# A partner swap moved from DMA to TensorE, a score matmul cut in two, a bias matmul on 33 rows: one kernel, two layers

## The reference

```python
# first layer: the relative bias, one row per head
off = np.arange(3 * blk)[None, :] - blk - np.arange(blk)[:, None]
bt = rel_bias[_t5_bucket(off * dil)]            # 32 buckets, 12 heads
...
# second layer: rotary positions on 16 of the 64 channels of q and k
x1, x2 = xr[..., : ROT_DIM // 2], xr[..., ROT_DIM // 2:]
rot = jnp.concatenate([x1 * c - x2 * s, x2 * c + x1 * s], axis=-1)
...
# second layer: scores of 128 queries, masked by chunks of 64 keys
scores = jnp.einsum('bqhmd,bkhmd->bhmqk', qb, kb).astype(jnp.float32) * scale
scores = jnp.where(mask[None, None, None], scores, -jnp.inf)
p = jax.nn.softmax(scores, axis=-1)
w = p[:, :, 0] - lam * p[:, :, 1]
```

## Time and profile before

| what | value |
|---|---|
| median of 3 runs | 3016.0 us (3014.78 to 3016.84) |
| profiled execution, its own time | 3014.78 us |
| its span, first to last instruction | 3012.7 us |
| TensorE matmuls busy | 2937.9 us, 98% |
| VectorE / ScalarE / GpSimd busy | 52% / 36% / 12% |
| mean granted TensorE clock | 0.996 |

### The profile page before, as it was taken

The page is one execution under the profiler, slowest core; times in us unless marked ns, Lnnn a source line. Parts: engine busy times, 40 slices in busy tenths (PEclk is TensorE's granted clock), DMA queues, the critical chain, the costliest instruction groups (busy, mean ns, idle before and its releaser), DMA issues.

```text
span 3012.7 us, 38881 instructions
## 1 busy us (share of the span) xinstructions
PE 2937.9 (98%) x16147; PEld 2493.6 (83%) x16147; DVE 1558.4 (52%) x2184; ACT 1071.6 (36%) x2306; POOL 371.8 (12%) x439
## 2 busy tenths in 40 slices
PE   7999999999999999999999999999999999999998
PEld 5788888888888888888878888888888888888887
DVE  5466666667674224131257555444544478743553
ACT  4443453454443213233332341121112144313553
POOL 0132222332231100000000000000000021101211
PEclk9999999999999999999999999999999999999999
DMA  3211111111012111111363321111111141111101
GB/s 121 74 53 53 43 55 41 46 43 36 26 42 66 50 63 37 66 43 57 116 232 107 125 99 63 43 42 56 44 54 43 56 135 58 71 41 67 41 29 43
DMA packets 60783, 194.33 MB, mean 65 GB/s; under 512 B 8352, under 2 KB 16416, under 8 KB 51392
## 3 DMA queue, kind: packets, MB, share of 16 engines
q1 hardware_dynamic: 58320, 189.19, 18.0%
q10 hardware_dynamic: 2288, 2.67, 0.3%
HBM read 156.80 MB, written 33.98 MB: 63 GB/s over the span
## 4 chain that ended last, share of the span: by engine, by line
PE 91%; DVE 4%; ACT 2%; issue 1%; DMA 1%; POOL 0%; SPq 0%; POOLq 0%; ACTq 0%; DVEq 0%
PE ps L2532 23%; PE ps L2534 23%; PE ps L2533 23%; PE ps L745 3%; PE ps L751 3%; PE ps L1759 1%; PE ps L1722 1%; PE ps L757 1%; PE ps L782 1%; PE ps L776 1%; PE ps L3410 1%; PE ps L788 1%; PE ps L728 1%; PE ps L797 1%; PE ps L796 1%
## 5 line engine op out<-in xcount | busy, mean ns | idle before, releaser
L2532 PE MATMUL ps<-r,r 128*128 128x512 f32 (+4 forms) x2992 | 1165.1, 389 | 20.3 <-DVE ar L3661 5.1
L2534 PE MATMUL ps<-r,r 128*128 128x512 f32 (+4 forms) x2992 | 1111.3, 371 | 0.0
L2533 PE MATMUL ps<-r,r 128*128 128x512 f32 (+4 forms) x2992 | 1108.9, 371 | 0.0
L2532 PEld LDWEIGHTS ps<-r,r 128*128 128x128 f32 (+1 forms) x2992 | 562.4, 188 | 105.6 <-issue 9.7
L2534 PEld LDWEIGHTS ps<-r,r 128*128 128x128 f32 (+1 forms) x2992 | 560.5, 187 | 99.4
L2533 PEld LDWEIGHTS ps<-r,r 128*128 128x128 f32 (+1 forms) x2992 | 562.7, 188 | 79.4 <-issue 0.7
L2532 PE MATMUL ps<-r 128*128 128x512 f32 x512 | 199.7, 390 | 0.8 <-DVE r L2521 0.8
L2534 PE MATMUL ps<-r 128*128 128x512 f32 x512 | 199.2, 389 | 0.0
L2533 PE MATMUL ps<-r 128*128 128x512 f32 x512 | 199.2, 389 | 0.0
L2792 DVE TENSOR_TENSOR ar<-ar,ps 128x512 f32<-128x512 f32 x224 | 150.8, 685 | 89.7 <-PE ps L2534 89.7
L2516 ACT ACTIVATE r<-ar 128x2048 fp32r<-128x2048 f32 x48 | 91.7, 1910 | 275.4 <-PE ps L2534 252.3
(11 more groups left out here) (331 smaller groups left out, 3887.8 us busy)
## 6 DMA issues: line engine op xcount, KB each, us to landing
ar<-wst SPq DMA_DIRECT2D x72, 1024.0 KB, 4.8
ar<-wst SPq DMA_DIRECT2D x56, 512.0 KB, 4.0
ar<-x SPq DMA_DIRECT2D x16, 512.0 KB, 6.0
ar<-sc_g SPq DMA_DIRECT2D x32, 256.0 KB, 4.6
sc_h<-ar SPq DMA_DIRECT2D x32, 256.0 KB, 2.0
sc_x<-ar SPq DMA_DIRECT2D x16, 512.0 KB, 2.7
ar<-sc_x SPq DMA_DIRECT2D x16, 512.0 KB, 3.9
sc_b<-ar SPq DMA_DIRECT2D x24, 260.0 KB, 2.0
```

Of the source, the lines that this page charges most:

```text
L2532: t.do.matmul(o, l[0], r[0], start=first, stop=False)
L2533: t.do.matmul(o, l[0], r[1], start=False, stop=False)
L2534: return t.do.matmul(o, l[1], r[0], start=False, stop=last)
```

## The change

Four edits.

1. The bias matmuls take 33 rows of both operands in place of 128.
2. The partner channels of the rotary step are no longer moved by DMA. A constant 128 by 128 matrix `permT` (one more slice of the `rope` input, loaded in stage 6's queue) holds the swap with its sign, and a new function `rotated` multiplies it with `rp` on TensorE, one matmul of 352, 336 or 512 columns per piece, into banks 4 to 7. VectorE's sine product reads that bank. The sine table loses its sign. The 80 DMAs from ScalarE's queue and the two clears of `rturn` are gone. `rotated` for piece j stands two pieces behind the projection of piece j; the last two stand behind the first and the second value piece.
3. A score cut that crosses the first masked key is cut there too, so that the masked keys have a matmul of their own, and the mask covers exactly that matmul's columns.
4. `lqk` and the tables have a semaphore of their own, `rope_in`.

```diff
@@ pe_bias
-t.do.matmul(bank(6 + n % 2)[:, 0:384], bc(rb[:, n:n + 1], 128, 128), oh[:, n // 4, :], ...)
+t.do.matmul(bank(6 + n % 2)[:, 0:384], bc(rb[0:33, n:n + 1], 33, 128), oh[0:33, n // 4, :], ...)
@@ sp_ff
-sp.do.dma_start(lqk, lam["lqk"].partition_broadcast(P)).then_inc(*lru_in.tick("lqk"))
+sp.do.dma_start(permT, rope[2][:, 0:128]).then_inc(*rope_in.tick("perm"))
+sp.do.dma_start(lqk, lam["lqk"].partition_broadcast(P)).then_inc(*rope_in.tick("lqk"))
@@ rope
+def rope_bank(k):
+    return small_bank(len(lru_keys) + rope_keys.index(k))
+
+def rotated(t, k):
+    i = rope_keys.index(k)
+    t.wait_ge(pj_act, k)
+    t.wait_ge(rope_in, "lqk")
+    if i >= 4:
+        t.wait_ge(rope_dve, ("sin", *rope_keys[i - 4]))
+    w = piece(k)[1]
+    t.do.matmul(rope_bank(k)[:, 0:w], permT, rp[i % 2][:, 0:w], start=True, stop=True).then_inc(*rope_mm.tick(k))
+
 def pe_rope(t):
-    for _ in begun["k"]:
-        pass
-    for _ in pe_cols3(t, "q", 0, (1, 2)):
-        pass
+    for k in rope_keys[:2]:
+        rotated(t, k)
+    for i, _ in enumerate(begun["k"]):
+        rotated(t, rope_keys[2 + i])
+    for i, _ in enumerate(pe_cols3(t, "q", 0, (1, 2))):
+        rotated(t, rope_keys[10 + i])
@@ act_rope
-if i < 2:
-    a.wait_ge(filled, "mask")
-a.wait_ge(pj_act, k)
-for s_, (to, of) in enumerate(((0, 8), (8, 0), (64, 72), (72, 64))):
-    a.do.dma_start(rturn[i % 2][to:to + 8, 0:w], rp[i % 2][of:of + 8, 0:w]).then_inc(*rope_turned[i % 2].tick((*k, s_)))
@@ dve_rope
-v.wait_ge(rope_turned[i % 2], (*k, 3))
-v.do.tensor_tensor(d, rturn[i % 2][:, 0:w], sinT[:, pos:pos + w], ALU.mult)...
+v.wait_ge(rope_mm, k)
+v.do.tensor_tensor(d, rope_bank(k)[:, 0:w], sinT[:, pos:pos + w], ALU.mult)...
@@ pe_values
+if (sl, i) == (0, 0):
+    rotated(t, rope_keys[-2])
 if (sl, i) == (0, 1):
+    rotated(t, rope_keys[-1])
     stage_left(t, "pe", 7)
@@ scores
-cuts.append((k0, k1))
+cuts += [(k0, k1)] if k1 <= lo or k0 >= lo else [(k0, lo), (lo, k1)]
...
-o = t.do.matmul(dst[m][:, max(lo - k0, 0):], negr[rows_, :], oner[rows_, 0:k1 - max(lo, k0)], start=False, stop=True)
+o = t.do.matmul(dst[m], negr[rows_, :], oner[rows_, 0:k1 - k0], start=False, stop=True)
@@ pool_mask
-p.do.memset(rturn[0], 0.0)
-p.do.memset(rturn[1], 0.0).then_inc(*pool_step.tick())
-p.wait_ge(pool_step, pool_step.n)
```

More of the change, by code:

```diff
@@ L816, in pe_bias @@
                     t.wait_ge(bias_row, n - 2)
-                t.do.matmul(bank(6 + n % 2)[:, 0:384], bc(rb[:, n:n + 1], 128, 128), oh[:, n // 4, :], start=True, stop=True).then_inc(*bias_mm.tick(n))
+                t.do.matmul(bank(6 + n % 2)[:, 0:384], bc(rb[0:33, n:n + 1], 33, 128), oh[0:33, n // 4, :], start=True, stop=True).then_inc(*bias_mm.tick(n))
                 yield
@@ L2551, in program @@
         meta_in = flow("meta_in", [0], 16)
-        lqk = A(C0 + 1280, 256)
+        permT, lqk = A(C0 + 1152, 128), A(C0 + 1280, 256)
+        rope_in = flow("rope_in", ["perm", "lqk", "cos", "sin"], 16)
         XB = [A(27648, 8, 128), A(39488, 8, 1040)[:, :, 912:1040]]
@@ L2880, in program @@
         GT = [A(Q0 + 10456 + 532 * i, 512) for i in range(2)]
-        lru_in = flow("lru_in", ["conv", "lqk"] + [(g, n) for g in range(2) for n in range(8)] + ["cos", "sin"], 16)
+        lru_in = flow("lru_in", ["conv"] + [(g, n) for g in range(2) for n in range(8)], 16)
         coef_a, coef_v = flow("coef_a", ["abs", "exp", "ln", "lam"]), flow("coef_v", ["rate", "sum", "lam"])
@@ L2934, in program @@
         lru_a = [flow(f"lru_a{q}", [(ct, n) for ct in (q, q + 2) for n in ("a", "th", "sqrt")]) for q in range(2)]
-        rope_turned = [flow(f"rope_turned{q}", [(*k, s_) for k in rope_keys[q::2] for s_ in range(4)], 16) for q in range(2)]
+        rope_mm = flow("rope_mm", rope_keys)
         rope_dve = flow("rope_dve", [(n, *k) for k in rope_keys for n in ("sin", "out")])
@@ L3147, in dve_lambda @@
         def dve_lambda(v):
-            v.wait_ge(lru_in, "lqk")
+            v.wait_ge(rope_in, "lqk")
             v.do.tensor_tensor(lqk[:, 0:64], lqk[:, 0:64], lqk[:, 64:128], ALU.mult)
@@ L3197, in program @@
         rp = [A(vO + 2080 + 512 * i, 512) for i in range(2)]
-        rturn = [A(vO + 3104 + 512 * i, 512) for i in range(2)]
         vv = A(vO, 9, 512)
-        def pe_rope(t):
-            for _ in begun["k"]:
-                pass
-            for _ in pe_cols3(t, "q", 0, (1, 2)):
-                pass
+        def rope_bank(k):
[8 more added lines that the diff above has]
+            t.do.matmul(rope_bank(k)[:, 0:w], permT, rp[i % 2][:, 0:w], start=True, stop=True).then_inc(*rope_mm.tick(k))
+        def pe_rope(t):
+            for k in rope_keys[:2]:
[4 more added lines that the diff above has]
+                rotated(t, rope_keys[10 + i])
         begun = {}
@@ L3237, in dve_rope @@
                 r_ = rp[i % 2][:, 0:w]
-                v.wait_ge(lru_in, "sin")
-                v.wait_ge(filled, "mask")
-                v.wait_ge(rope_turned[i % 2], (*k, 3))
-                v.do.tensor_tensor(d, rturn[i % 2][:, 0:w], sinT[:, pos:pos + w], ALU.mult).then_inc(*rope_dve.tick(("sin", *k)))
+                v.wait_ge(rope_in, "sin")
+                v.wait_ge(rope_mm, k)
+                v.do.tensor_tensor(d, rope_bank(k)[:, 0:w], sinT[:, pos:pos + w], ALU.mult).then_inc(*rope_dve.tick(("sin", *k)))
                 v.do.tensor_tensor(r_, r_, cosT[:, pos:pos + w], ALU.mult).then_inc(*dve_step.tick())
@@ L3247, in sp_rope @@
             for n, key, dst in ((0, "cos", cosT), (1, "sin", sinT)):
-                sp.do.dma_start(dst, rope[n]).then_inc(*lru_in.tick(key))
+                sp.do.dma_start(dst, rope[n]).then_inc(*rope_in.tick(key))
             for j in range(38, 42):
@@ L3885, in constants @@
     ang = pos[:, None] * inv[None, :]
-    rope = np.zeros((2, 128, 1040), f)
+    rope = np.zeros((3, 128, 1040), f)
     rope[0] = 1
@@ L3890, in constants @@
             rope[0, 64 * b + d] = rope[0, 64 * b + 8 + d] = np.cos(ang[:, d])
-            rope[1, 64 * b + d], rope[1, 64 * b + 8 + d] = -np.sin(ang[:, d]), np.sin(ang[:, d])
+            rope[1, 64 * b + d] = rope[1, 64 * b + 8 + d] = np.sin(ang[:, d])
+            rope[2, 64 * b + 8 + d, 64 * b + d] = -1
+            rope[2, 64 * b + d, 64 * b + 8 + d] = 1
     return cst.reshape(128, 768), msk, oh, rope
```

## The result

The changed kernel takes 3039.2 us (median of 4 runs, 3038.16 to 3039.99); the kernel before took 3015.9 us in the same comparison (4 runs). The ratio is 1.0075, 95% interval 1.0062 to 1.0088: 23.3 us slower. The record holds 13 executions of the changed kernel in all, from 3035.9 to 3040.0 us. The forecast was 19.7 us slower, 3035.6 us, with a range of 3028 to 3043. The profiled execution took 3038.45 us, with a span of 3036.6 us, 23.9 us over the span before.

A forecast was written before the change was run, and what follows sets the result against it. TensorE, busy for 98% of the span, was taken as the bound. Swap 13.9, scores 3.3 and bias 2.5 us sum to 19.7 us, which on the median of 3016.0 us gives 3035.6 us; range 3028 to 3043.

The forecast's parts named there:

- The swap: Rotary stage: 20 rotations, 8256 columns on TensorE, add 13.9 us; the removed DMAs return 0 us.
- The price per column: TensorE: a plain float32 matmul between split ones costs 1.67 ns per column, both recorded passes together.
- The slack reckoned for the new round trip: Rotary stage, TensorE to VectorE to ScalarE and back: 1.4 us for k and at the stage boundary, so no stall.
- B: Rotary stage: rotations wait, each stalling TensorE by 1 us, 20 us on top, about 3055 us; chance 12%.
- C: Rotary stage: rotations are free, their 13.9 us hiding in gaps, 5.8 us remaining, 3021.8 us; chance 6%.
- The scores: Last stretch: the extra score cuts cost 4.5 us over four heads, 3.3 us of it on the chain.
- The floor of 0.11 us per pass: Score and mask matmuls: a short pass takes at least 0.11 us, so a masked 64-key piece costs 0.22.
- Rival D: Scores: the cut gains through equal extents, at most 0.06 us per item, 2 us; 3030 us; chance 3%.
- The bias: Bias matmuls: 33 rows treated as 64, 0.41 us per change of rows and back, together 2.5 us.
- upper bound of 4.9 us: Bias matmuls: the most the edit could cost, all 12 matmuls paying 0.41 us each.
- the wait swallows the three ahead of it: Bias stretch: three bias matmuls stand before TensorE's wait of 3.01 us, which absorbs their changes of rows.
- about 2 us either way: TensorE's clock: a dip more or less at 1.2 GHz, falling to the new pauses, shifts the time by about 2 us.

The follow-up runs named there:

- the run with 128 keys: Kernel before with an extra score cut 128 keys from the end in blocks 1, 2, 5 and 6, mask unchanged: 3016.2 against 3016.2 us.
- A filled wait on 128 rows: Kernel before, bias on 128 rows, with six unread float32 matmuls of 256 columns in TensorE's wait near 98 us: 3017.1 against 3016.8 us.

## Why the prediction was right, and which term was mis-sized

**The bound.** TensorE bounds the rotary stage, as the earlier trace rows said: every added column came out in the time, once and twice.

**The swap: 13.9 us, measured 13.8 to 13.9 on TensorE and +14.4 in the medians.** The price per column from a bias matmul in the first layer held for 20 matmuls in the second. The removed DMAs returned nothing. The slack reckoned for the new round trip was there, and also with rotations twice as long. Rivals B and C are out.

**The scores: 3.3 us, measured +3.1 in the medians, about 2.6 on TensorE.** Item by item the chain shows the added 0.11 us that was worked out for 400 keys. The distances on TensorE add 0.20 for 144 keys (1.25 against 1.05), as worked out too. The floor of 0.11 us per pass, which was read off the 16 key pieces, is what makes the cut cost; the run with 128 keys shows it by its absence. Rival D is out.

**The bias: 2.5 us, measured +5.5.** This is the mis-sized term, and it went past the upper bound of 4.9 us that the prediction gave it. Its mechanism held nearly throughout: 33 rows are treated as 64, a change there and back costs 0.40 us, the wait swallows the three ahead of it (the pair behind the wait, charged 0.41, cost 0.06), and at full clock the changes come to 2.0 us. What the term left out is TensorE's clock. The prediction had it as "about 2 us either way", with no place, and without asking which stretch of the queue already had pauses. It has a place: the bias stretch, where pauses of 1.38 and 3.01 us stood already. With 33 rows a spell of 3.4 us at 1.2 GHz appeared at 84 us, in all three profiles with all twelve on 33 rows and in none of the others, the one on 64 rows included, 1.7 us; and the spell behind the wait was 6.8 us long in both unfilled profiles with all twelve on 33 rows (10.2 on 64). In the nine unfilled profiles whose matmuls right behind the wait are on 128 or 96 rows it was absent in four, 3.4 us long in three and 6.8 in two: 2.6 us on average.

So the account by medians is 14.4 + 3.1 + 5.5 = 23.0 us, against 23.3 measured. That it closes to 0.3 us is luck: each term is known to about 3 us at best, and rotations and cuts together gave 15.6, not 17.5. Of the bias part about 2.0 are changes of rows, 1.7 the spell at 84 us, and 1.8 are left; half of 6.8 - 2.6 us, the longer spell behind the wait, would be 2.1. That last figure is argued from averages, not shown by itself: the spells vary between executions of the same kernel, a profile shows one execution each, and 1.8 us is less than the interval of the 5.5. The same holds in part for the 1.7: the run on 64 rows makes the same changes and kept its clock at 84 us. Taken together the three unfilled profiles with a change at all twelve (33, 33 and 64 rows) each lost 5.1 us to 10.2 us of low clock, the nine others 1.3 on average. Whether the spell at 84 us follows from the changes of rows alone or from these together with the wait in front of it wasn't tried. A filled wait on 128 rows should give back those 1.3 us on average, too little for the medians to show.

The profiled execution of before was one without the spell behind the wait. Beside it, a profile of the changed kernel charges the change with a delay that the kernel before had in its second profile, and that five of the nine profiles counted above have. It didn't move the forecast, but it misled my first reading of the profile after.

The total of 23.3 us lies in the range because the range added the upper bounds of all terms and 2 us of clock, while on TensorE only the bias term went over its bound. The size of the clock's share was not foreseen.

## What to carry to other kernels

On a queue that is full, price an added matmul by its columns from the distance between two starts, check that its passes have at least 128 columns, and look whether it uses another part of the array than its neighbours: here 1.67 ns per float32 column, a floor of 0.11 us per pass, and 0.40 us for a change of rows and back. Leaving out rows of a matmul among full ones saves nothing and can cost. Before a difference between two profiles is put down to the change, profile the unchanged kernel a second time; the clock of one stretch can differ.

## What I had not expected of the hardware

A matmul on 96 rows went through at the price of 128 (no change in the time), one on 33 at the price of 64 (1.50). And the clock behind a pause of TensorE isn't the same in each execution: the kernel before, profiled twice, kept 2.4 GHz after a wait of 3.01 us and fell to 1.2 GHz for 3.4 us after one of 3.49; a variant alike up to there kept it after 3.52 us, and another (rotations and cuts on 128 rows) lost it for 6.8 us around one of 2.94. So the length of this wait doesn't say whether the clock falls. With 2.7 us of unread matmuls in the wait it stayed up behind it in both runs.
